# Regrouping the tokens of a feed-forward stage to 512, 320 and 256, with one joint product for the smallest group

## Chip, cores and metric

The kernel runs on one core of one Trainium2 chip. The metric is device time in microseconds (us) of one execution, as the median of several runs. The engines are named as the profile names them: PE is TensorE (matmul), PEld its weight loads, DVE VectorE, ACT ScalarE, POOL GpSimd, SP the engine that issues most DMAs.

## What is computed

One decoder layer over 1088 tokens (1024 of a prompt and 8 samples of 8), with D = 1024 and a hidden width of 2816. The stages are a half-step feed-forward layer, a token mixer (a gated linear recurrence and gated linear attention), cross-attention over 256 memory tokens, a second half-step feed-forward layer, and a final norm:

```
x = x + 0.5 * swiglu_ffn(x, p['ffn1_norm'], p['ffn1_w_gate'], p['ffn1_w_up'], p['ffn1_w_down'])
x = x + mix                       # token mixer
x = x + cross_attend(x, mem_k, mem_v, ...)
x = x + 0.5 * swiglu_ffn(x, p['ffn2_norm'], p['ffn2_w_gate'], p['ffn2_w_up'], p['ffn2_w_down'])
y = rmsnorm(x, p['final_norm'])

def swiglu_ffn(x, g, w_gate, w_up, w_down):
    h = rmsnorm(x, g)
    return (jax.nn.silu(h @ w_gate) * (h @ w_up)) @ w_down
```

Everything is float32. The kernel reaches this precision with split operands: a value v is held as a rounded half `hi` and a rest `lo = v - hi`, and a product is made of three matmuls, w_hi by x_hi, w_hi by x_lo, and w_lo by x_hi.

## The kernel before

**Layout.** x lies in SBUF as `x[128, 8, 1088]`: features on the partitions in 8 blocks k, tokens along the row. A product for one block of 128 output features runs over the 8 blocks k with three matmuls each (`split_mm`, lines L1736, L1737, L1738). The moving operand of each is the activation, so a matmul has as many columns as its group has tokens. The tokens are in three groups n = 0, 1, 2 of 384, 384 and 320 (`NS`), in the whole kernel.

**A feed-forward stage** (`ffn(f)`, f = 0 and 1, on every engine) is 11 iterations `it`; each takes two hidden blocks ft = 0, 1 of 128 features. Three parts follow each other on PE:

- Six gate/up steps s. A step is one hidden block for one group: a gate product u = 0 and an up product u = 1, 8 x 3 matmuls each, into the PSUM banks 4 + 2(s%2) + u. In iteration 0 the order is (ft, n) = (0,0), (1,0), (0,1), (1,1), (0,2), (1,2); in the others (0,0), (0,1), (0,2), (1,0), (1,1), (1,2).
- The work on a finished step. ACT makes the silu of the gate (L849, `sil`), DVE multiplies it with the up product in PSUM (L1296, `hf`), then splits it: a cast to `h_hi` (L1300) and a subtraction to `h_lo` (L1302). Before it takes the banks of step s again, PE waits for the multiplication of two steps before.
- Down products: for n = 0, 1, 2 and each of 8 output blocks m, 6 matmuls into bank m%4; DVE adds half of it to x (L1310, `add`). The product m may start only when the addition of four products before is done, since it takes that bank. The products of group n wait for the `h_lo` of that group.

**Weights.** Each iteration loads six tiles of 128 x 1024 (slots 0 to 3 gate and up, 4 and 5 down). ACT rounds each to `w_hi` (L772, `prep`), POOL subtracts to `w_lo` (L696, `low`). Slots 2 and 3 of the next iteration are loaded when the last gate/up step is done. In stage f = 0, while it = 0 to 9, ACT and POOL also split six tiles of the later stages' weights in each iteration (L783 and L701, `stage_prep` and `stage_low`), three of them right behind slots 2 and 3.

**Norms.** A group's norm is: squares (ACT, L810), sums of eight squared rows (DVE L1144 and L1145, or POOL L730 and L732), sums over partitions (PE, L1763), root (ACT, L823) and reciprocal (DVE, L1137), a spread of the scale to all partitions (PE, L1785), then the scaled rows (DVE, L1215; L1169 in the mixer; L1244 for the final norm) and their split (ACT L838, DVE L1227). In iteration 0 the norms of groups 1 and 2 stand between the steps; in the last iteration the next stage's norm of group 0 stands between the additions of groups 1 and 2, the final norm's rows of group 0 between the additions of group 2.

**What sets the order.** Every engine's program is written out by hand, in order; the engines meet at semaphores. Nothing is rearranged by a scheduler.

## Time and profile before

| what | value |
|---|---|
| median of 3 runs | 2379.21 us (2378.66 to 2383.64) |
| span of the profiled execution | 2379.0 us |
| mean granted TensorE clock | 0.995 |
| PE busy | 2343.7 us (99%), 14996 matmuls |
| DVE busy | 1062.5 us (45%) |
| ACT busy | 494.6 us (21%) |
| POOL busy | 519.1 us (22%) |

The span runs from the first to the last instruction and is 0.2 us below the median of the runs. Stage f = 0 lies from 0 to about 811 us, the mixer and the attention up to about 1567 us, stage f = 1 behind them up to the last additions at about 2364 us. Matmuls are pipelined, so the busy time of one overlaps that of the next: how long one costs is read from the distance between two starts, not from its duration. L12 is line 12 of the kernel.

### The profile page before, as it was taken

What the parts mean: (1) busy time and instruction counts of PE and PEld (TensorE: products, weight loads), DVE (VectorE), ACT (ScalarE), POOL (GpSimd) and SP (SyncE); (2) the same over time, 40 slices, a digit from 0 to 9 for tenths busy, and PEclk for the clock granted to TensorE, in tenths of its full rate; (3) what the DMA queues carried; (4) which work ended last, traced back from release to release, by engine and by line L of the source; (5) the groups of instructions that cost most, each with busy time, mean ns of one, the idle gap of its engine ahead of it and who ended that gap; (6) DMA issues with size and microseconds to landing.
All of it is one profiled execution on the core that took longest, in us unless ns stands there. A gap on an engine that the chain in (4) does not pass through costs nothing. (4 is left out here: it accounts for less than half of the span.)

```text
span 2379.0 us, 36652 instructions
## 1 busy us (share of the span) xinstructions
PE 2343.7 (99%) x14996; PEld 2285.3 (96%) x14996; DVE 1062.5 (45%) x1696; ACT 494.6 (21%) x697; POOL 519.1 (22%) x239
## 2 busy tenths in 40 slices
PE   7999999999999999999999999999999999999998
PEld 7999999999999989899889999799999999999998
DVE  6434334444334574565642423444443344443345
ACT  4222212122211241321410221331111011111101
POOL 2444334344432000000001000022221222221121
PEclk9999999999999999999999999999999999999999
DMA  4554454454452465666678376731101010111112
GB/s 158 213 212 168 159 194 175 151 212 168 159 194 89 156 214 182 212 222 240 231 261 316 145 254 252 276 110 54 53 36 53 35 53 35 53 35 53 35 36 76
DMA packets 89475, 352.50 MB, mean 148 GB/s; under 512 B 8944, under 2 KB 16432, under 8 KB 79152
## 3 DMA queue, kind: packets, MB, share of 16 engines
q1 hardware_dynamic: 89104, 351.12, 40.3%
q8 instruction: 64, 1.05, 0.2%
q10 hardware_dynamic: 288, 0.18, 0.0%
q14 instruction: 19, 0.16, 0.0%
HBM read 280.54 MB, written 70.72 MB: 148 GB/s over the span
## 5 line engine op out<-in xcount | busy, mean ns | idle before, releaser
L1736 PE MATMUL ps<-a_hi,w_sb 128*128 128x384 f32 (+1 forms) x2112 | 691.6, 327 | 6.6 <-DVE a_lo L1227 4.6
L1738 PE MATMUL ps<-a_hi,w_sb 128*128 128x384 f32 (+1 forms) x2112 | 689.9, 327 | 0.0
L1737 PE MATMUL ps<-a_lo,w_sb 128*128 128x384 f32 (+1 forms) x2112 | 689.7, 327 | 0.0
L696 POOL TENSOR_TENSOR w_sb<-w_raw,w_sb 128x1024 fp32r<-128x1024 f32 x132 | 317.7, 2415 | 1066.4 <-ACT w_sb L772 1066.4
L1736 PEld LDWEIGHTS ps<-a_hi,w_sb 128*128 128x128 f32 x2112 | 397.7, 188 | 8.3 <-issue 3.5
L1737 PEld LDWEIGHTS ps<-a_lo,w_sb 128*128 128x128 f32 x2112 | 397.8, 188 | 0.0
L1738 PEld LDWEIGHTS ps<-a_hi,w_sb 128*128 128x128 f32 x2112 | 397.6, 188 | 0.0
L1310 DVE SCALAR_TENSOR_TENSOR x<-ps,x 128x384 f32<-128x384 f32 (+1 forms) x528 | 279.2, 534 | 199.7 <-PE ps L1738 199.7
L1296 DVE TENSOR_TENSOR hf<-sil,ps 128x384 f32<-128x384 f32 x132 | 70.1, 531 | 646.9 <-ACT sil L849 646.9
L1736 PE MATMUL ps<-h_hi,w_sb 128*128 128x384 f32 (+1 forms) x1056 | 344.7, 326 | 0.0
L1738 PE MATMUL ps<-h_hi,w_sb 128*128 128x384 f32 (+1 forms) x1056 | 344.2, 326 | 0.0
L1737 PE MATMUL ps<-h_lo,w_sb 128*128 128x384 f32 (+1 forms) x1056 | 344.1, 326 | 0.0
L849 ACT ACTIVATE sil<-ps 128x384 f32<-128x384 f32 x132 | 62.4, 473 | 1125.8 <-PE ps L1738 1125.7
L1302 DVE TENSOR_TENSOR h_lo<-hf,h_hi 128x384 fp32r<-128x384 f32 x132 | 239.5, 1815 | 4.6
L1736 PEld LDWEIGHTS ps<-h_hi,w_sb 128*128 128x128 f32 x1056 | 198.3, 188 | 0.3 <-DVE x L1310 0.3
L1737 PEld LDWEIGHTS ps<-h_lo,w_sb 128*128 128x128 f32 x1056 | 198.2, 188 | 0.0
L1738 PEld LDWEIGHTS ps<-h_hi,w_sb 128*128 128x128 f32 x1056 | 198.2, 188 | 0.0
L730 POOL TENSOR_TENSOR sq<-sq 128x768 f32<-128x768 f32 (+2 forms) x18 | 31.8, 1769 | 691.9 <-ACT sq L810 691.9
L772 ACT ACTIVATE w_sb<-w_raw 128x1024 fp32r<-128x1024 f32 x132 | 139.1, 1056 | 101.8 <-DMA w_raw<-in_ffn_gate 92.7
L701 POOL TENSOR_TENSOR st_w<-st_raw,st_w 128x1024 fp32r<-128x1024 f32 x60 | 145.2, 2448 | 48.8 <-ACT st_w L783 48.8
L1736 PE MATMUL ps<-mo_hi,w_sb 128*128 128x384 f32 (+1 forms) x384 | 125.7, 327 | 0.7 <-DVE mo_lo L1676 0.7
L1738 PE MATMUL ps<-mo_hi,w_sb 128*128 128x384 f32 (+1 forms) x384 | 125.1, 326 | 0.0
(262 smaller groups left out, 2717.2 us busy)
## 6 DMA issues: line engine op xcount, KB each, us to landing
w_sb<-split SPq DMA_DIRECT2D x148, 1024.0 KB, 5.2
split<-st_w SPq DMA_DIRECT2D x60, 1024.0 KB, 4.1
st_raw<-in_mix_tiles SPq DMA_DIRECT2D x60, 512.0 KB, 5.9
w_raw<-in_ffn_gate SPq DMA_DIRECT2D x44, 512.0 KB, 3.6
w_raw<-in_ffn_up SPq DMA_DIRECT2D x44, 512.0 KB, 4.4
w_raw<-in_ffn_down SPq DMA_DIRECT2D x44, 512.0 KB, 4.3
kc<-in_cache_k SPq DMA_DIRECT2D x5, 1024.0 KB, 8.5
kc<-in_cache_v SPq DMA_DIRECT2D x4, 1024.0 KB, 9.6
```

Source lines behind the costliest of these rows:

```text
L696: nc.gpsimd.tensor_tensor(w_lo_sb[:, slot_, :], raw[:, slot_, :], w_hi_sb[:, slot_, :].bitcast(F32), ALU.subtract)\
L701: nc.gpsimd.tensor_tensor(st_w[:, j % 3, 1, :], st_raw[:, j % 3, 1, :], st_w[:, j % 3, 0, :].bitcast(F32), ALU.subtract)\
L730: nc.gpsimd.tensor_tensor(buf[:, 0:2, 0:p.N], buf[:, 0:2, 0:p.N], buf[:, 2:4, 0:p.N], ALU.add).then_inc(pool_half, 1)
L772: nc.scalar.activation(w_hi_sb[:, slot_, :], raw[:, slot_, :], ACT.Copy).then_inc(w_hi, 1)
L849: nc.scalar.activation(sil[:, s % 2, 0:N], ps[:, 4 + 2 * (s % 2), 0:N], ACT.Silu).then_inc(silu_done, 1)
L1296: nc.vector.tensor_tensor(hf[:, s % 2, 0:N], sil[:, s % 2, 0:N], ps[:, b + 1, 0:N], ALU.mult).then_inc(h_done, 1)
L1302: nc.vector.tensor_tensor(h_lo[ft][:, tokens(n)], hf[:, s % 2, 0:N], h_hi[ft][:, tokens(n)].bitcast(F32), ALU.subtract)\
L1310: nc.vector.scalar_tensor_tensor(out=x[:, m, tokens(n)], in0=ps[:, m % 4, 0:NS[n]], scalar=0.5, in1=x[:, m, tokens(n)], op0=ALU.mult, op1= ...
L1736: nc.tensor.matmul(dst, w_h, x_h, start=start, stop=False)
L1737: nc.tensor.matmul(dst, w_h, x_l, start=False, stop=False)
L1738: return nc.tensor.matmul(dst, w_l, x_h, start=False, stop=stop)
```

## The change

In the two feed-forward stages and the final norm the groups are now 512, 320 and 256 tokens (`FNS`, `ftokens`); mixer and attention keep 384, 384 and 320.

The two halves of group 2's activations lie behind each other in one tile `a_both`. Its gate and up products are made by `joint_mm`: one matmul of w_hi with both halves, 512 columns into one bank (columns 0 to 255 are w_hi by x_hi, 256 to 511 w_hi by x_lo), and one of w_lo with x_hi, 256 columns into the first half. The halves of the bank are added afterwards: ACT copies columns 256 to 511 of both banks to `part`, DVE adds them onto columns 0 to 255, and only then come the silu and the multiplication.

`sil` is one buffer instead of two. The cast and the subtraction of step 5 (`hidden(5, 1, 2)`) stand behind the eight additions of group 0, not ahead of them. What the norms wait for follows the new borders: the norm of group 0 of stage f = 1 waits for the attention output of groups 0 and 1, that of group 1 for part of group 2 and, with its second half, all of it. The squares get buffers that fit.

```diff
+FOFFS = [0, 512, 832]
+FNS = [512, 320, 256]
@@ wait_source
             elif kind == "ffn2":
-                eng.wait_ge(evicted, FIRST["co", n] + 8)
+                eng.wait_ge(evicted, FIRST["co", min(n + 1, 2)] + (4 if n == 1 else 8))
@@ sync: x is loaded by the new groups
-                sp.dma_start(x[:, 4 * h:4 * h + 4, tokens(0)], ...
+                sp.dma_start(x[:, 4 * h:4 * h + 4, ftokens(0)], ...
@@ scalar, norm_squares
                     elif q == 0:
                         wait_source(act, kind, n)
+                    elif (kind, n) == ("ffn2", 1):
+                        act.wait_ge(evicted, FIRST["co", 2] + 8)
@@ scalar, ffn
                 def step(q0, s, first):
                     _, n = ffn_step(first, s)
                     act.wait_ge(gu_done, f * GATE_UP_STEPS + q0 + s + 1)
-                    if f or not first or s >= 2:
-                        act.wait_ge(h_done, f * GATE_UP_STEPS + q0 + s - 1)
-                    N = NS[n]
-                    nc.scalar.activation(sil[:, s % 2, 0:N], ps[:, 4 + 2 * (s % 2), 0:N], ACT.Silu).then_inc(silu_done, 1)
+                    if f or not first or s >= 1:
+                        act.wait_ge(h_done, f * GATE_UP_STEPS + q0 + s)
+                    N = FNS[n]
+                    b = 4 + 2 * (s % 2)
+                    if n == 2:
+                        ft, _ = ffn_step(first, s)
+                        nc.scalar.activation(part[:, :, :], ps[:, b:b + 2, N:2 * N], ACT.Copy).then_inc(part_out, 1)
+                        act.wait_ge(whole_out, f * 2 * ITS + q0 // 6 * 2 + ft + 1)
+                    nc.scalar.activation(sil[:, 0:N], ps[:, b, 0:N], ACT.Silu).then_inc(silu_done, 1)
@@ vector, ffn
+                    def hidden(s, ft, n):
+                        if f or not first:
+                            dve.wait_ge(down_done, X + Q * it - Q + KT * (n + 1))
+                        dve.wait_ge(h_done, G + q0 + s + 1)
+                        nc.vector.tensor_copy(h_hi[ft][:, ftokens(n)], hf[:, s % 2, 0:FNS[n]]).then_inc(hhi_done, 1)
+                        dve.wait_ge(hhi_done, G + q0 + s + 1)
+                        nc.vector.tensor_tensor(h_lo[ft][:, ftokens(n)], hf[:, s % 2, 0:FNS[n]], h_hi[ft][:, ftokens(n)].bitcast(F32), ALU.subtract)\
+                          .then_inc(hid_done, 1)
+
                         b = 4 + 2 * (s % 2)
+                        if n == 2:
+                            dve.wait_ge(part_out, f * 2 * ITS + 2 * it + ft + 1)
+                            nc.vector.tensor_tensor(ps[:, b:b + 2, 0:N], part[:, :, :], ps[:, b:b + 2, 0:N], ALU.add).then_inc(whole_out, 1)
                         dve.wait_ge(silu_done, G + q0 + s + 1)
...
+                        nc.vector.tensor_tensor(hf[:, s % 2, 0:N], sil[:, 0:N], ps[:, b + 1, 0:N], ALU.mult).then_inc(h_done, 1)
+                        if s < 5:
+                            hidden(s, ft, n)
                     for n in range(3):
+                        if n == 1:
+                            hidden(5, 1, 2)
@@ vector, cross-attention output of group 2
-                    if n == 2 and j == 4:
+                    if n == 2 and j == 6:
                         norm_sum("ffn2", 1, 0)
@@ tensor
+            def joint_mm(dst, w_h, w_l, x_both, start, stop):
+
+                N = x_both.shape[2]
+                nc.tensor.matmul(dst[:, 0:2 * N].rearrange("p (a n) -> p a n", a=2), w_h, x_both, start=start, stop=False)
+                return nc.tensor.matmul(dst[:, 0:N], w_l, x_both[:, 0], start=False, stop=stop)
@@ tensor, ffn
-                                ins = split_mm(ps[:, 4 + 2 * (s % 2) + u, 0:NS[n]], w_hi_sb[:, w, c], w_lo_sb[:, w, c],
-                                               a_hi[n][:, k, :], a_lo[n][:, k, :], k == 0, k == KT - 1)
+                                if n == 2:
+                                    ins = joint_mm(ps[:, b, :], w_hi_sb[:, w, c], w_lo_sb[:, w, c], a_both[:, :, k, :], k == 0, k == KT - 1)
+                                else:
+                                    ins = split_mm(ps[:, b, 0:FNS[n]], w_hi_sb[:, w, c], w_lo_sb[:, w, c],
+                                                   a_hi[n][:, k, :], a_lo[n][:, k, :], k == 0, k == KT - 1)
```

**PE, a gate product of group 2 in a middle iteration.** `w_sb` is the weight, a_hi_67 and a_lo_68 are the halves of group 2. Before:

```order
L1736 MATMUL ps<-a_hi_67,w_sb 128x320
L1737 MATMUL ps<-a_lo_68,w_sb 128x320
L1738 MATMUL ps<-a_hi_67,w_sb 128x320
L1736 MATMUL ps<-a_hi_67,w_sb 128x320
L1737 MATMUL ps<-a_lo_68,w_sb 128x320
L1738 MATMUL ps<-a_hi_67,w_sb 128x320
```

And now, for the same two blocks k and one more:

```order
L1783 MATMUL ps<-a_both,w_sb 128x512
L1784 MATMUL ps<-a_both,w_sb 128x256
L1783 MATMUL ps<-a_both,w_sb 128x512
L1784 MATMUL ps<-a_both,w_sb 128x256
L1783 MATMUL ps<-a_both,w_sb 128x512
L1784 MATMUL ps<-a_both,w_sb 128x256
```

Two matmuls stand where three stood; a group of 256 in the old form would also have taken three.

**DVE, from the last gate/up step of iteration 0 through the additions.** (The middle iterations have the same order, with register instructions between.) Before:

```order
L1296 TENSOR_TENSOR hf<-sil,ps 128x320 [waits hid_done,silu_done]
L1300 CAST h_hi_72<-hf 128x320 [waits h_done]
L1302 TENSOR_TENSOR h_lo_73<-hf,h_hi_72 128x320 [waits hhi_done]
L1310 SCALAR_TENSOR_TENSOR x<-ps,x 128x384 [waits down_done] x16
L1310 SCALAR_TENSOR_TENSOR x<-ps,x 128x320 [waits down_done] x8
```

Now:

```order
L1334 TENSOR_TENSOR ps<-part,ps 128x2x256 [waits part_out]
L1338 TENSOR_TENSOR hf<-sil,ps 128x256 [waits hid_done,silu_done]
L1350 SCALAR_TENSOR_TENSOR x<-ps,x 128x512 [waits down_done] x8
L1311 CAST h_hi_73<-hf 128x256 [waits h_done]
L1313 TENSOR_TENSOR h_lo_74<-hf,h_hi_73 128x256 [waits hhi_done]
L1350 SCALAR_TENSOR_TENSOR x<-ps,x 128x320 [waits down_done] x8
L1350 SCALAR_TENSOR_TENSOR x<-ps,x 128x256 [waits down_done] x8
```

An addition in PSUM has come in ahead of the multiplication, and cast and subtraction have moved past the eight additions of group 0.

**ACT, the last gate/up step of a middle iteration.** Before:

```order
L849 ACTIVATE sil<-ps 128x384
L772 ACTIVATE w_sb<-w_raw 128x1024
L845 REGISTER_ALU
L849 ACTIVATE sil<-ps 128x320
L772 ACTIVATE w_sb<-w_raw 128x1024 x2
```

Now:

```order
L877 ACTIVATE sil<-ps 128x320
L793 ACTIVATE w_sb<-w_raw 128x1024
L868 REGISTER_ALU
L875 ACTIVATE part<-ps 128x512
L876 REGISTER_ALU
L877 ACTIVATE sil<-ps 128x256
L793 ACTIVATE w_sb<-w_raw 128x1024 x2
```

The copy to `part` is new, ahead of the silu and of the weights of slots 2 and 3.

## Rows read from the trace of the kernel before

**Rows 1.** Page, costliest groups: operation, count | busy us, mean ns | idle.

```profile
L1736 PE MATMUL ps<-a_hi,w_sb 128*128 128x384 f32 (+1 forms) x2112 | 691.6, 327 | 6.6 <-DVE a_lo L1227 4.6
```

**Rows 2.** Windows: stretch; PE, PEld, DVE, ACT, POOL busy; clock; DMA.

```profile
97.00:736.00 639.00, 639.00 (x3884) 639.00 (x3883) 266.21 (x377) 130.10 (x162) 263.19 (x110) 1.00 0.48 182
1575.00:1590.00 15.00, 12.53 (x61) 12.12 (x60) 8.79 (x14) 7.20 (x10) 5.00 (x2) 0.77 0.01 2
```

**Rows 3.** Timeline, PE: start, length; pairs at 256, 384, 512 columns.

```profile
1221.05 0.28 PE L1736 MATMUL ps<-xm_hi,w_sb 128*128 128x256 f32 x1
...
1224.65 0.28 PE L1736 MATMUL ps<-xm_hi,w_sb 128*128 128x256 f32 x1
...
384.39 0.33 PE L1736 MATMUL ps<-a_hi,w_sb 128*128 128x384 f32 x1
...
387.51 0.33 PE L1736 MATMUL ps<-a_hi,w_sb 128*128 128x384 f32 x1
...
1235.67 0.39 PE L1900 MATMUL ps<-w_sb,xm_hi 128*128 128x512 f32 x1
...
1240.43 0.39 PE L1900 MATMUL ps<-w_sb,xm_hi 128*128 128x512 f32 x1
```

**Rows 4.** Timeline, stage f = 0, down products of it = 5; last row of it = 7.

```profile
428.65 0.34 PE L1736 MATMUL ps<-h_hi,w_sb 128*128 128x384 f32 x1
...
433.12 0.56 DVE L1310 SCALAR_TENSOR_TENSOR x<-ps,x 128x384 f32<-128x384 f32 x1 [0.48 <-PE ps L1738]
...
433.65 4.79 POOL L696 TENSOR_TENSOR w_sb<-w_raw,w_sb 128x1024 fp32r<-128x1024 f32 x2 [7.92 <-ACT w_sb L772]
438.39 7.11 POOL L701 TENSOR_TENSOR st_w<-st_raw,st_w 128x1024 fp32r<-128x1024 f32 x3
...
580.24 7.12 POOL L701 TENSOR_TENSOR st_w<-st_raw,st_w 128x1024 fp32r<-128x1024 f32 x3
```

**Rows 5.** Timeline, DVE beside POOL in iteration 0; last row without POOL, it = 5.

```profile
61.73 7.27 POOL L701 TENSOR_TENSOR st_w<-st_raw,st_w 128x1024 fp32r<-128x1024 f32 x3 [7.60 <-ACT st_w L783]
...
65.98 0.75 DVE L1300 CAST h_hi<-hf 128x384 fp32r<-128x384 f32 x1
...
66.76 2.65 DVE L1302 TENSOR_TENSOR h_lo<-hf,h_hi 128x384 fp32r<-128x384 f32 x1
...
430.27 0.49 DVE L1302 TENSOR_TENSOR h_lo<-hf,h_hi 128x320 fp32r<-128x320 f32 x1
```

**Rows 6.** Timeline, start of the program, up to PE's first gate matmul.

```profile
7.96 1.48 ACT L810 ACTIVATE sq_b<-x 128x1536 f32<-128x1536 f32 x1 [0.76 <-DMA x<-in_x]
...
11.08 1.44 PE L1763 MATMUL ps<-cst,sq_b 128*128 128x1 f32 x6 [0.74 <-DVE sq_b L1145]
...
14.83 2.19 DVE L1215 SCALAR_TENSOR_TENSOR frow<-x,vec,ps 128x384 f32<-128x384 f32 x4 [1.74 <-PE ps L1785]
...
18.07 0.66 PE L1736 MATMUL ps<-a_hi,w_sb 128*128 128x384 f32 x1 [3.28 <-DVE a_lo L1227]
```

**Rows 7.** Timeline, start of stage f = 1, POOL and PE.

```profile
1575.13 5.00 POOL L696 TENSOR_TENSOR w_sb<-w_raw,w_sb 128x1024 fp32r<-128x1024 f32 x2 [8.14 <-ACT w_sb L772]
...
1577.98 0.83 PE L1763 MATMUL ps<-cst,sq_b 128*128 128x1 f32 x6 [1.10 <-DVE sq_b L1145]
1580.18 0.69 PE L1736 MATMUL ps<-a_hi,w_sb 128*128 128x384 f32 x1 [1.37 <-POOL w_sb L696]
```

**Rows 8.** Timeline, iteration 0 of f = 1: DVE, then PE in step 4.

```profile
1604.28 2.66 DVE L1302 TENSOR_TENSOR h_lo<-hf,h_hi 128x384 fp32r<-128x384 f32 x1
...
1613.11 0.41 PE L1736 MATMUL ps<-a_hi,w_sb 128*128 128x320 f32 x1 [0.64 <-DVE a_lo L1227]
```

**Rows 9.** Timeline, PE, the mixer's first matmul.

```profile
811.20 0.41 PE L1736 MATMUL ps<-xn_hi,w_sb 128*128 128x384 f32 x1 [0.73 <-issue]
```

**Rows 10.** Timeline, DVE, last iteration of f = 1 and the last rows.

```profile
2347.21 0.96 DVE L1144 TENSOR_TENSOR sq<-sq 128x768 f32<-128x768 f32 x1 [0.52 <-ACT sq L810]
...
2369.19 5.83 DVE L1244 SCALAR_TENSOR_TENSOR yb<-x,vec,ps 128x384 f32<-128x384 f32 x12
```

More of the change, by code:

```diff
@@ L35 @@
 NMAX = 384
+FOFFS = [0, 512, 832]
+FNS = [512, 320, 256]
+FMAX = 512
 NPROMPT = [384, 384, 256]
@@ L476, in tokens, with ftokens, group @@
             return slice(OFFS[n], OFFS[n] + NS[n])
+        def ftokens(n):
+            return slice(FOFFS[n], FOFFS[n] + FNS[n])
+        def group(kind, n):
+            return ftokens(n) if kind in ("ffn1", "ffn2", "fin") else tokens(n)
         def norm_source(kind, n, q):
@@ L484, in norm_source @@
                 return osb[:, :, 0:N]
-            return (memx if kind == "mem" else x)[:, 4 * q:4 * q + 4, slice(0, N) if kind == "mem" else tokens(n)]
+            return (memx if kind == "mem" else x)[:, 4 * q:4 * q + 4, slice(0, N) if kind == "mem" else group(kind, n)]
         GATE_UP_STEPS = 6 * ITS
```

75 lines of the change are left out of this document (39 added, 36 removed).

## The prediction, made before the result was known

> **What bounds the kernel now.** I read the windows first. From 97 to 736 us, nine whole iterations of stage f = 0, PE is busy 639.00 of 639.00 us at full granted clock, DVE 266, POOL 263 [rows 2]. So in the loops PE alone sets the time. A change there is worth what it takes off PE's stream, as long as nobody starts to make PE wait. Outside the loops PE waits at a few places, and these depend on how wide group 0 is [rows 6 to 10].
>
> The price of a matmul is the distance of two starts. At 256 columns 30 matmuls take 3.60 us, 120.0 ns each; at 384 columns 18 take 3.12 us, 173.3 ns; at 512 columns 21 take 4.76 us, 226.7 ns [rows 3]. The clock granted there is full, 2.4 GHz. All three are (columns + 32) / 2.4 GHz: each matmul has a fixed part of 13.3 ns, whatever its width. An iteration has 432 matmuls and 156,672 columns, which gives 71.04 us.
>
> **A. The joint product: -9.4 us.** The columns per block k stay 3 x 1088; the matmuls go from 9 to 8. The x2112 of [rows 1] is 44 hidden blocks x 2 products x 8 k x 3 groups, so 704 are saved: 704 x 13.3 ns = 9.4 us, 0.43 us in each of 22 iterations. Down products keep their count. No row shows a moving operand in two pieces of 256 columns. Dearest, the two pieces cost like two matmuls, and A is 0; nothing in the rows lets it fall below -9.4. I take -9.4, since output and count of columns are those of an ordinary 512-column matmul [rows 3].
>
> The Trainium skill, page "TensorE: Matmul & The Clock Gate", section "Back-to-back issue gap", speaks against this gain: it gives N/2.4 + 2.5 ns at full clock. By it A would be 704 x 2.5 ns = 1.8 us. The trace disagrees, with 13.3 ns at three widths.
>
> ACT's copy and DVE's addition lengthen the way from a finished step to its h by about 1.3 us (0.6 + 0.7, taken from 512-wide neighbours of the 0.56 us of a 384-wide operation [rows 4]). They cost nothing: PE needs those banks again only after the next step, 7 us or more in the middle iterations. ACT has `prep` and `stage_prep` queued behind, and slots 2 and 3 are in the air until after that.
>
> **B. Last h behind the additions: +8.6 us.** The critical place is the middle iterations of f = 0. Call U the start of the down products, 428.65 in [rows 4]. A product m of group 0 takes 6 x 226.7 ns = 1.36 us, so group 0 ends at U + 10.88. DVE starts an addition 0.31 us behind the product's end (433.12 is U + 4.47, the fourth product ended at U + 4.16 [rows 4]). The last one, 0.70 us at 512 tokens less 0.06 of overlap, lets the cast begin at U + 11.83, which is 440.48.
>
> What POOL does then is [rows 4]: two `low` to 438.4, then three `stage_low` of 2.4 us, starting at 438.39, 440.75 and 443.1. And [rows 5] shows how DVE fares beside such a row of POOL operations. The cast (0.75 us in place of 0.36) got through between the second and the third. The subtraction had to wait for the whole third, and ended 0.42 us behind it (66.76 + 2.65 against 69.00); alone it takes 0.49 at 320 columns. Additions that read PSUM are not held up (0.56 us at 433.12, in the middle of POOL's work [rows 4]).
>
> So: the cast gets through at 440.8, the subtraction ends 0.28 us (0.42 less 128/0.96 ns for the smaller width) behind the second `stage_low`, which the cast pushes to 443.27: 443.55. The addition 0 of group 1 starts 0.08 us before that, takes 0.49 and ends at 443.96, PE could go on at 444.01. PE wants it for product m = 4 of group 1, at U + 10.88 + 4 x 6 x 146.7 ns = U + 14.40 = 443.05 (320 columns cost 352/2.4 ns by [rows 3]). The stall is 0.96 us, in nine iterations (it = 1 to 9): 8.6 us. Before, the same step ran at U + 1.3, ahead of POOL's work. In f = 1 there is no `stage_low`, and POOL is done at U + 10: free. In iteration 0 the weights come later than U + 11.8: free.
>
> Bounds: where POOL is as early as at 580.24 (U = 570.85, so its first `stage_low` ends at U + 11.79 [rows 4]), the cast misses the gap, the subtraction ends behind the third operation, and the stall is 0.96 + 2.05 = 3.0 us. Otherwise the ends in the nine iterations lie at 11.97 to 12.28. From below, the subtraction gets in right behind the cast: no stall. So 0 to 27 us, and I take 0.96 each.
>
> **C. The start: +4.0 us.** The first two loads of x grow by a third. The second landed at about 7.96, with the first 1.57 MB in all [rows 6]; at 2.10 MB it is +1.5. Squares, 1.48 us for 1536 elements, +0.45; the two sums +0.4; PE's column sums and spread, 8 small matmuls for 6, +0.9 over both; four scaled rows (2.19 us [rows 6]) and the first split, +0.8. Together +4.1 on the first gate matmul, 18.07 before. The pairs then arrive slower (+0.3), and a wait of 0.36 us for slots 2 and 3 goes, since the first step is 2.6 us longer. +4.0; between +3 and +5.
>
> **D. Start of f = 1: -3.7 us.** Before, PE waited twice, 1.10 and 1.37 us idle and some more to refill, for the sums of group 1 and for the weights of slots 2 and 3 [rows 7], 3.1 us in all, and then ran at 1.2 GHz: the window from 1575 has a mean clock of 0.77 [rows 2], worth about 2.1 us. The product that covers the waits grows from 4.16 to 5.44 us twice. The sums are then in time; POOL's 5 us pair starts 0.9 us later and ends at 1581.1, against 1579.6 when PE gets there. 1.5 us remain, and no other wait lies beside it: at 1613.11 a single wait of 0.64 [rows 8] did not lower the clock. 1.5 against 5.2 is -3.7; with the clock still falling -1.6.
>
> **E. Step 4 of iteration 0, twice: +1.0 us.** PE stood 0.8 us there (0.64 idle [rows 8]) for the split of group 2. The step before is 1.3 us shorter, the split itself gets 1.1 us shorter, but four blocks k of step 4 last 1.4 us and not 1.8, and every pair is late: +1.1. If the subtraction ahead (2.66 us beside POOL [rows 8]) comes ahead of POOL's operation, 2.2 us are gained, and this is -0.8. The margin shrinks to about 0.03 us in f = 1, and turns in f = 0, where a shorter step 4 then waits 0.7 us for its banks. +1.1 and -0.1; range -1 to +3.
>
> **F. Into the mixer: +1.1 us.** In the last iteration of each stage, group 0 ends 2.56 us later and groups 1 and 2 are 1.28 us shorter each. DVE's chain from the end of group 0 to the next stage does not shorten as much. For f = 0 the chain to the mixer's first matmul (811.20 [rows 9], 18.55 us behind the end of group 0) shortens to 17.1. +2.56 - 1.45 = +1.1; 0 to +2.
>
> **G. The tail: +3.1 us.** In f = 1 the squares of group 0 wait for the last h too. They end 3.5 us after the end of group 0 (2.1 before), the sum of 0.96 us [rows 10] becomes 1.24, and PE waits 2.1 us at m = 4. Behind it narrower rows of the final norm (12 rows in 5.83 us [rows 10] become 5.2) give most of it back: the distance from the end of group 0 to the last row stays near 30 us (+0.5). With the 2.56: +3.1; +2 to +4. A fourth spread column in the attention adds 0.3.
>
> **Sum.** -9.4 + 8.6 + 4.0 - 3.7 + 1.0 + 1.1 + 3.1 + 0.3 = +5.0. The profiled 2379.0 us become 2384.0, and the median, 0.2 above it, 2384.2.
>
> **Rivals.**
> - *The cover holds*: B is 0. It decides whether the subtraction ends before U + 13.9; for it speaks only that iteration 0 showed one case of the pattern [rows 5]. 2384.2 - 8.6 = 2375.6. Chance 0.20.
> - *The cast misses the gap* in several iterations, 2.05 us each: four give 2392, all nine 2402.6. It needs `stage_low` 0.4 us earlier than usual; one of nine was. 0.15.
> - *The joint matmul saves nothing* (two pieces cost like two): 2384.2 + 9.4 = 2393.6. 0.08.
> - *Fixed part of 2.5 ns*: A shrinks to 1.8 us, 2391.8. The three widths are against it. 0.02. This is the Trainium skill's rule named above.
> - *Faster*: B is 0 and start and tail cost half (3.5 less): 2372.1. 0.05.
>
> **How the numbers follow.** The forecast has 0.50, by itself 2380.5 to 2387.5. A measurement can tell about 0.2% from no change, 4.8 us: faster is below 2374.4, slower above 2384.0. The forecast's half splits 0.28 slower, 0.22 same; the first rival 0.14 same, 0.06 faster; the next three, 0.25, are slower; the last 0.05 faster. Faster 0.11, same 0.36, slower 0.53. The range takes in the first rival and most of the second and third: 2374.5 to 2394.
>
> **What would show it.** A: in a middle iteration of f = 1, 70.6 us instead of 71.1 between two first gate matmuls, and 346.7 ns for a pair of joint matmuls. B: one wait of PE of nearly 1 us in each of nine iterations of f = 0, ended by an addition (L1350), with a subtraction (L1313) of some 2.4 us before it; iterations of 71.6 us. C: first gate matmul at 22.2. D: no clock of 1.2 GHz near 1585. F, G: waits of PE at m = 4 of the last iterations. I am wrong if f = 0 runs as fast as f = 1, or if the pair costs 360 ns.

## The result, and the profile of the changed kernel

The changed kernel takes 2393.8 us (median of 4 runs, 2393.1 to 2395.4) against 2380.0 us before (4 runs, 2378.7 to 2383.6): ratio 1.0050, 95% interval 1.0036 to 1.0064. It is slower by 0.5%. The direction was right, and the time lies inside the range (2374.5 to 2394) by 0.2 us; the size was not right: +5.0 us forecast, +13.8 measured. The profiled span is 2392.7 us against 2379.0, so +13.7 is what the traces have to explain. One execution of the kernel with three repairs (below) took 3878 us at a mean granted clock of 0.557 and is left out of that kernel's numbers.

The page, costliest groups, now has the plain product of groups 0 and 1 in L1776 and the joint one in L1783 and L1784 (the rows answer to [rows 1]):

```profile
L1776 PE MATMUL ps<-a_hi,w_sb 128*128 128x320 f32 (+1 forms) x1408 | 494.5, 351 | 6.3 <-DVE a_lo L1255 4.0
...
L1783 PE MATMUL ps<-a_both,w_sb 128*128 128x512 f32 x704 | 250.9, 399 | 2.3 <-DVE a_both L1255 1.7
...
L1784 PE MATMUL ps<-a_both,w_sb 128*128 128x256 f32 x704 | 197.7, 281 | 0.0
```

704 matmuls are gone, as the change says. The windows (columns as in [rows 2]) are f = 0 beyond its first iteration, the start of f = 1 and a stretch of the tail:

```profile
103.00:750.00 647.00, 639.97 (x3595) 572.38 (x3595) 259.03 (x395) 140.81 (x180) 270.85 (x110) 1.00 0.47 179
...
1580.00:1595.00 15.00, 13.42 (x67) 11.14 (x65) 3.29 (x5) 5.11 (x6) 5.52 (x3) 1.00 0.32 112
2360.00:2375.00 15.00, 12.96 (x91) 12.80 (x91) 10.85 (x21) 5.72 (x5) 3.85 (x3) 0.89 0.00 1
```

In f = 0 PE is no longer busy all the time: 7.0 of 647 us are missing. The view of PE's waits from 100 to 760 us has one line, the sum, the number and the longest of them:

```profile
PE ps L1776 <- DVE x L1350: 7.0, 9, 1.1
```

So that an account can be made, here are PE's first matmuls of iterations 1 and 10 of both stages, and the attention's last one (timeline):

```profile
102.59 0.40 PE L1776 MATMUL ps<-a_hi,w_sb 128*128 128x512 f32 x1
...
750.55 0.40 PE L1776 MATMUL ps<-a_hi,w_sb 128*128 128x512 f32 x1
...
1580.67 0.31 PE L1778 MATMUL ps<-mo_hi,w_sb 128*128 128x320 f32 x1
...
1659.62 0.40 PE L1776 MATMUL ps<-a_hi,w_sb 128*128 128x512 f32 x1
...
2298.20 0.40 PE L1776 MATMUL ps<-a_hi,w_sb 128*128 128x512 f32 x1
```

The same places before: 96.85, 736.75, 1566.69, 1649.25, 2289.15 us. With the terms of the prediction put into the same stretches (A is -0.43 an iteration; E lies in the first and in the fourth stretch):

| stretch | before | after | measured | forecast |
|---|---|---|---|---|
| start to iteration 1 | 96.85 | 102.59 | +5.7 | +3.5 |
| f = 0, iterations 1 to 9 | 639.90 | 647.96 | +8.1 | +4.7 |
| to the attention's last matmul | 829.94 | 830.12 | +0.2 | +1.0 |
| to iteration 1 of f = 1 | 82.56 | 78.95 | -3.6 | -3.0 |
| f = 1, iterations 1 to 9 | 639.90 | 638.58 | -1.3 | -3.9 |
| iteration 10 and tail | 89.9 | 94.5 | +4.6 | +2.7 |
| sum | 2379.0 | 2392.7 | +13.7 | +5.0 |

The short stretches are not the same in every profile. The kernel with a measuring row (below) is the changed kernel up to its end: its first gate matmul comes at 23.80 us (24.27 here) and its iteration 1 at 102.18. In the third stretch lie the mixer and the attention, which the change leaves nearly alone, and a fall of the clock. The window 1190 to 1230 us, before and then after:

```profile
1190.00:1230.00 40.00, 39.23 (x385) 37.13 (x384) 15.10 (x39) 8.54 (x14) 0.00 (x0) 0.91 0.61 225
```

```profile
1190.00:1230.00 40.00, 39.38 (x450) 37.05 (x450) 12.52 (x41) 6.50 (x14) 1.31 (x2) 0.96 0.52 188
```

Over the kernels with the new groups the third stretch lies between 829.5 and 831.7 us. The mixer's first matmul shows how much of it the change made (timeline, after; before [rows 9]):

```profile
826.41 0.41 PE L1776 MATMUL ps<-xn_hi,w_sb 128*128 128x384 f32 x1 [0.93 <-issue]
```

That is 75.86 us behind the start of iteration 10, against 74.45 before.

**The waits in f = 0.** DVE, POOL and PE (timeline) in iteration 2, whose down products start at 221.85 us (the rows answer to [rows 4, 5]):

```profile
233.00 0.69 DVE L1350 SCALAR_TENSOR_TENSOR x<-ps,x 128x512 f32<-128x512 f32 x1 [0.58 <-PE ps L1778]
233.60 0.56 DVE L1311 CAST h_hi<-hf 128x256 fp32r<-128x256 f32 x1
234.20 2.52 DVE L1313 TENSOR_TENSOR h_lo<-hf,h_hi 128x256 fp32r<-128x256 f32 x1
236.64 2.29 DVE L1350 SCALAR_TENSOR_TENSOR x<-ps,x 128x320 f32<-128x320 f32 x5
...
226.87 4.78 POOL L717 TENSOR_TENSOR w_sb<-w_raw,w_sb 128x1024 fp32r<-128x1024 f32 x2 [6.30 <-ACT w_sb L793]
231.59 7.37 POOL L722 TENSOR_TENSOR st_w<-st_raw,st_w 128x1024 fp32r<-128x1024 f32 x3
...
237.18 0.41 PE L1776 MATMUL ps<-h_hi,w_sb 128*128 128x320 f32 x1 [0.70 <-DVE x L1350]
```

The row of POOL merges three `stage_low` of about 2.46 us. The cast gets through near the end of the first (231.59 + 2.46 = 234.05), the subtraction is held for the whole second one and ends at 236.72, the addition behind it at 237.1, and PE stands. All nine iterations show this order. With U, as in the prediction, for the start of the down products: the cast starts at U + 11.75, and the first `stage_low` ends between U + 12.01 and U + 12.56. In f = 1, where POOL has no `stage_low`, the same two instructions are short:

```profile
1931.45 0.28 DVE L1311 CAST h_hi<-hf 128x256 fp32r<-128x256 f32 x1
1931.77 0.42 DVE L1313 TENSOR_TENSOR h_lo<-hf,h_hi 128x256 fp32r<-128x256 f32 x1
```

**The joint product.** PE, first and sixteenth 512-column matmul of two products that follow each other (timeline):

```profile
1890.42 0.39 PE L1783 MATMUL ps<-a_both,w_sb 128*128 128x512 f32 x1
...
1895.72 0.40 PE L1783 MATMUL ps<-a_both,w_sb 128*128 128x512 f32 x1
```

Fifteen pairs take 5.30 us, 353 ns each, where 226.7 + 120.0 = 346.7 were forecast [rows 3]. In iteration 0 of f = 1 the same instructions, in the same order, run faster (PE, two 512-column matmuls, sixteen pairs apart):

```profile
1627.59 0.39 PE L1783 MATMUL ps<-a_both,w_sb 128*128 128x512 f32 x1
...
1633.13 0.39 PE L1783 MATMUL ps<-a_both,w_sb 128*128 128x512 f32 x1
```

Sixteen pairs in 5.54 us are 346 to 347 ns each. So the joint pair has two steady prices in one and the same kernel; all the middle iterations have the dear one.

**The start** (answers to [rows 6]). POOL, DVE, PE:

```profile
12.62 5.18 POOL L717 TENSOR_TENSOR w_sb<-w_raw,w_sb 128x1024 fp32r<-128x1024 f32 x2 [12.17 <-ACT w_sb L793]
...
12.89 2.71 DVE L1173 TENSOR_TENSOR sq_e<-sq_e 128x512 f32<-128x512 f32 x1
...
24.27 0.77 PE L1776 MATMUL ps<-a_hi,w_sb 128*128 128x512 f32 x1 [4.04 <-DVE a_lo L1255]
```

**Step 4 in f = 0, start of f = 1, step 4, and tail** (PE; answers to [rows 7, 8, 10]), then DVE's last rows of the final norm:

```profile
68.04 0.50 PE L1783 MATMUL ps<-a_both,w_sb 128*128 128x512 f32 x1 [0.45 <-DVE a_both L1255]
...
73.22 0.50 PE L1783 MATMUL ps<-a_both,w_sb 128*128 128x512 f32 x1 [0.65 <-DVE hf L1338]
...
1595.58 0.50 PE L1776 MATMUL ps<-a_hi,w_sb 128*128 128x512 f32 x1 [1.29 <-POOL w_sb L717]
...
1625.99 0.51 PE L1783 MATMUL ps<-a_both,w_sb 128*128 128x512 f32 x1 [0.54 <-DVE a_both L1255]
...
2362.07 1.02 PE L1809 MATMUL ps<-cst,sq 128*128 128x1 f32 x8 [2.04 <-DVE sq L1173]
...
2384.03 5.04 DVE L1272 SCALAR_TENSOR_TENSOR yb<-x,vec,ps 128x320 f32<-128x320 f32 x12
```

One wait is left at the start of f = 1, and the clock stays at 1.00 from 1580 (0.77 before [rows 2]). At the tail PE waits 2.04 us, and from 2360 the clock is 0.89.

### The profile page after: what moved, and what is told of

The parts are those of the page before. It is cut to its first block and busy times, and to the rows that moved or that the text cites. A ratio compares the mean times of both kernels' runs of the same rounds, so it can differ in the third digit from the quotient of the medians.

```text
span 2392.7 us, 35406 instructions
## 1 busy us (share of the span) xinstructions
PE 2342.2 (98%) x14292; PEld 2121.0 (89%) x14292; DVE 1048.5 (44%) x1740; ACT 519.8 (22%) x741; POOL 534.1 (22%) x239
## 5 line engine op out<-in xcount | busy, mean ns | idle before, releaser
L1776 PE MATMUL ps<-a_hi,w_sb 128*128 128x320 f32 (+1 forms) x1408 | 494.5, 351 | 6.3 <-DVE a_lo L1255 4.0
L1778 PE MATMUL ps<-a_hi,w_sb 128*128 128x320 f32 (+1 forms) x1408 | 492.5, 350 | 0.0
L1777 PE MATMUL ps<-a_lo,w_sb 128*128 128x320 f32 (+1 forms) x1408 | 492.5, 350 | 0.0
L1776 PE MATMUL ps<-h_hi,w_sb 128*128 128x512 f32 (+2 forms) x1056 | 347.9, 329 | 7.7 <-DVE x L1350 7.7
L1350 DVE SCALAR_TENSOR_TENSOR x<-ps,x 128x512 f32<-128x512 f32 (+2 forms) x528 | 278.9, 534 | 173.8 <-PE ps L1778 170.4
L1778 PE MATMUL ps<-h_hi,w_sb 128*128 128x512 f32 (+2 forms) x1056 | 346.3, 328 | 0.0
L1777 PE MATMUL ps<-h_lo,w_sb 128*128 128x512 f32 (+2 forms) x1056 | 345.9, 328 | 0.0
L1776 PEld LDWEIGHTS ps<-a_hi,w_sb 128*128 128x128 f32 x1408 | 264.9, 188 | 36.2 <-issue 4.3
L1778 PEld LDWEIGHTS ps<-a_hi,w_sb 128*128 128x128 f32 x1408 | 264.7, 188 | 28.6
L1777 PEld LDWEIGHTS ps<-a_lo,w_sb 128*128 128x128 f32 x1408 | 265.1, 188 | 27.7
L1783 PE MATMUL ps<-a_both,w_sb 128*128 128x512 f32 x704 | 250.9, 399 | 2.3 <-DVE a_both L1255 1.7
L1776 PEld LDWEIGHTS ps<-h_hi,w_sb 128*128 128x128 f32 x1056 | 200.0, 189 | 25.1 <-DVE x L1350 10.2
L1784 PE MATMUL ps<-a_both,w_sb 128*128 128x256 f32 x704 | 197.7, 281 | 0.0
L1313 DVE TENSOR_TENSOR h_lo<-hf,h_hi 128x512 fp32r<-128x512 f32 (+1 forms) x132 | 193.4, 1465 | 4.6
L1783 PEld LDWEIGHTS ps<-a_both,w_sb 128*128 128x128 f32 x704 | 132.2, 188 | 34.6 <-DVE a_both L1255 2.4
```

Source lines behind the costliest of these rows:

```text
L1313: nc.vector.tensor_tensor(h_lo[ft][:, ftokens(n)], hf[:, s % 2, 0:FNS[n]], h_hi[ft][:, ftokens(n)].bitcast(F32), ALU.subtract)\
L1350: nc.vector.scalar_tensor_tensor(out=x[:, m, ftokens(n)], in0=ps[:, m % 4, 0:FNS[n]], scalar=0.5, in1=x[:, m, ftokens(n)], op0=ALU.mult, o ...
L1776: nc.tensor.matmul(dst, w_h, x_h, start=start, stop=False)
L1777: nc.tensor.matmul(dst, w_h, x_l, start=False, stop=False)
L1778: return nc.tensor.matmul(dst, w_l, x_h, start=False, stop=stop)
L1783: nc.tensor.matmul(dst[:, 0:2 * N].rearrange("p (a n) -> p a n", a=2), w_h, x_both, start=start, stop=False)
```

## Experiments

All edits are to the changed kernel unless it says otherwise. Where an edit is given in words or with "...", it stands for a longer one. Each time is a median of several runs (the measuring row ran once), but each trace is of one execution.

### The last h back ahead of the additions

```
-                        if s < 5:
-                            hidden(s, ft, n)
+                        hidden(s, ft, n)
                     for n in range(3):
-                        if n == 1:
-                            hidden(5, 1, 2)
```

> The changed kernel with one part undone: the last h of an iteration is split into halves ahead of the additions again, in both stages. Theory (the late split is what makes PE wait): the nine waits of 0.7 to 1.3 us at the fifth product of group 1 in f = 0 are gone, an iteration of f = 0 lasts 71.0 us as one of f = 1 does (72.0 in the changed kernel), and the last iterations lose their waits at the same place: 9.4 us less in the loops and some 2 us at the tail, 2382 to 2385 us in all. Rival (the widths of the groups, 512 columns in group 0, are what makes DVE late): the waits move to another product of group 0 or 1 but stay near 1 us, 2392 to 2395 us.

2386.2 us, ratio to before 1.0025 (1.0015 to 1.0036). The view of PE's waits in f = 0 is empty. PE, iterations 1 and 10:

```profile
102.66 0.40 PE L1772 MATMUL ps<-a_hi,w_sb 128*128 128x512 f32 x1
...
741.24 0.40 PE L1772 MATMUL ps<-a_hi,w_sb 128*128 128x512 f32 x1
```

638.58 us for nine iterations, 70.95 each: 9.4 us less than 647.96. The rival falls. The late split costs 9.4 us in the loops of f = 0. The whole kernel gains less, 7.7 us by the medians, and the 2 us expected at the tail did not come: by the profiles the stretch between the loops got 1.6 us longer and the tail 0.8. The 1.6 us go with the clock in the attention (0.91 from 1190 to 1230 us, 0.96 in the changed kernel). At the tail PE is idle for 1.29 us where it was 2.04, but the clock from 2350 to 2360 falls to 0.76.

### POOL's operations moved away from the late split

```
                     if f == 0:
+                        pool.wait_ge(hid_done, 6 * it + 6)
                         for j in range(3, 6):
                             stage_low(it, j)
```

> The changed kernel; POOL waits in f = 0 for the last h's subtraction before it starts its second three stage_low operations, so that no long POOL operation runs beside DVE's cast and subtraction. Theory (the subtraction waits for a whole POOL operation): cast 0.28 and subtraction 0.42 us as in f = 1, no wait of PE at the fifth product of group 1, iterations of f = 0 at 70.95 us, 9.4 us less than the changed kernel, 2384.4 us. Rival (the order of DVE's work alone makes the addition late): the waits stay near 1 us, or are half as long, and the kernel stays above 2389.

2387.7 us, ratio 1.0028 (1.0018 to 1.0039). DVE and POOL at the same place:

```profile
232.12 0.28 DVE L1312 CAST h_hi<-hf 128x256 fp32r<-128x256 f32 x1
232.44 0.42 DVE L1314 TENSOR_TENSOR h_lo<-hf,h_hi 128x256 fp32r<-128x256 f32 x1
...
233.03 7.14 POOL L722 TENSOR_TENSOR st_w<-st_raw,st_w 128x1024 fp32r<-128x1024 f32 x3 [2.97 <-DVE h_lo L1314]
```

The split stays late, every iteration of f = 0 lasts 70.95 us, and PE has no wait. So it is not the order of DVE's work but POOL's operation beside the subtraction that makes the addition late. The 9.4 us expected off the loops came; by the profiles 3.0 us were lost again behind them, 1.4 between the loops (again with a clock of 0.91 from 1190 to 1230) and 1.6 at the tail (96.1 us from iteration 10 in place of 94.5), where the clock from 2350 to 2360 was 0.76.

The Trainium skill, page "SBUF — State Buffer", section "Who interferes with whom", says which pairs get in each other's way: a DVE instruction with two inputs in SBUF contends with a GpSimd instruction that reads SBUF, since its second input comes through a read interface that both share, and that sharing is an exclusive lock; a DVE instruction with at most one input in SBUF, outside the modes that take both ports, doesn't contend. By that rule the subtraction is held and an addition with one input in PSUM is not; the traces agree (subtraction 2.52 against 0.42 us; addition of 512 tokens 0.69 us beside POOL at 233.00 and 0.69 us at 1930.84, where POOL is idle).

### The late split alone, on the kernel before

The same edit as in the change, with groups of 384, 384, 320 and three matmuls per block.

> The kernel before with the late split alone (groups 384, 384, 320, three products). Group 0 of the down products ends at U + 8.3, the last addition at U + 9.2, PE wants the first addition of group 1 at U + 12.5. Theory (what the late split costs depends on where in POOL's row it falls): cast in the gap at U + 9.6, subtraction behind the first stage_low, ended near U + 12.3, addition 0.56 us, so PE waits 0.3 to 0.5 us in nine iterations, 71.4 to 71.6 us each in f = 0, and 71.10 in f = 1; with up to 1 us at the tail 2383 to 2386 us. Rival 1 (a late split costs 0.96 us wherever it falls): 72.1, 2389 us. Rival 2 (only 512 columns make it late): 71.10 and 2380.

2387.9 us, ratio 1.0035 (1.0022 to 1.0047). DVE, then POOL, in iteration 2 (down products from 216.58 us):

```profile
225.60 1.12 DVE L1283 CAST h_hi<-hf 128x320 fp32r<-128x320 f32 x1
226.75 2.57 DVE L1285 TENSOR_TENSOR h_lo<-hf,h_hi 128x320 fp32r<-128x320 f32 x1
...
226.46 7.46 POOL L701 TENSOR_TENSOR st_w<-st_raw,st_w 128x1024 fp32r<-128x1024 f32 x3
```

Nine waits, the first matmul behind each 0.58 to 0.76 us late, iterations of 71.79 to 71.99 us, 7.1 us in all. The mechanism is that of the theory (cast at the end of POOL's first pair, subtraction behind the first `stage_low`); the size was short by about half, since the two instructions end at 229.32, U + 12.7, and not at U + 12.3. Rival 2 falls; of the late split's price 512 columns are only a part. Rival 1 is not far off by its size (0.79 us an iteration measured, 0.96 by the rival); what speaks against it is the kernel with groups of 384, 448, 256 below, where the subtraction is held just as long (2.5 us) and PE doesn't wait.

### Gate and up of group 2 as three matmuls

> The changed kernel with gate and up of group 2 as three 256-column matmuls per block k again; ACT's copy and DVE's addition are gone. Theory (a matmul has a fixed part of 13.3 ns, but the joint one loses half of it again): three take 360.0 ns against 353.0 for the joint pair, so a middle iteration of f = 1 goes from 70.95 to 71.17 us and the kernel gets 4.9 us slower, near 2398.7. Rival 1 (the whole 13.3 ns is saved, and the 512-column groups lose it elsewhere): 71.38 us an iteration, 2403. Rival 2 (the joint matmul saves nothing): 70.95, and 2393.8 unchanged.

2399.9 us, ratio 1.0087 (1.0070 to 1.0104). In f = 1 an iteration takes 71.10 us, exactly as before the change, and not the 71.17, 71.38 or 70.95 expected. So the joint product is worth 0.147 us an iteration (71.10 less 70.95, before rounding), 3.2 us in 22, a third of the 9.4 of step A. The trace shows the parts of an iteration: the two hidden blocks' joint products take 11.30 us where the three-matmul ones take 11.52, 0.22 less, and each of the two rows of 48 matmuls of 512 columns behind a joint product takes 10.94 us in place of 10.91. The whole time came near the theory's 2398.7, but partly by luck: the loops account for 3.2 of the 6.1 us between the two medians.

### The joint matmul reads one piece

```
-        a_both, o = at("a_both", [P, 2, KT, FNS[2]], o, F32R)
+        a_both, o = at("a_both", [P, KT, 2 * FNS[2]], o, F32R)
```

> The changed kernel with both halves of a of group 2 side by side for each block k, so that the joint matmul reads one piece of 512 columns in place of two pieces of 256 that lie 8 KB apart. Theory T (reading two pieces costs 6 to 9 ns a matmul): the 512-column matmul falls from 236 to 226.7 ns, the pair from 353.0 to 346.7 or less, a middle iteration of f = 1 from 70.95 to 70.75, the kernel to 2389.4 us. Rival S (going from 256 to 512 columns and back costs it, whatever the layout): 353.0 ns, 70.95 us and 2393.8 stay.

Pairs of 353.0 ns and iterations of 70.95 us, as with two pieces: theory T falls. The time was 2399.0 us, ratio 1.0085 (1.0068 to 1.0101), 5 us above the changed kernel although its loops of f = 1 are the same and those of f = 0 0.8 us shorter. In the profile the difference lies where PE waits and the clock falls: 1.8 us at the start of f = 1 and 3.0 at the tail. The window 2360 to 2375 of this kernel:

```profile
2360.00:2375.00 15.00, 12.97 (x64) 12.71 (x63) 7.48 (x13) 5.55 (x6) 0.45 (x1) 0.66 0.00 1
```

0.66 against 0.89, and 0.90 against 1.00 from 1595 to 1610. Why all four runs of this kernel were above 2398 us was not found out.

### The wide matmuls first

```
-  for k: joint_mm(512 columns of w_hi; 256 columns of w_lo)
+  for k: 512 columns of w_hi
+  for k: 256 columns of w_lo
```

> The changed kernel with the order of the joint product changed: first its eight 512-column matmuls, then its eight 256-column ones, in place of one and one in turn. Rival S (each change from narrow to wide costs about 7 ns): the seven changes inside a product go, the wide ones take 226.7 ns and the narrow ones 120.0 (346.7 for both), an iteration of f = 1 lasts 70.75 us in place of 70.95, the kernel 2389.4. Theory T (two pieces cost it): the wide ones stay at 236 ns or more, and nothing changes, 2393.8.

PE, first 512-column matmul of two products in a row:

```profile
1891.75 0.39 PE L1784 MATMUL ps<-a_both,w_sb 128*128 128x512 f32 x1
...
1894.54 0.40 PE L1784 MATMUL ps<-a_both,w_sb 128*128 128x512 f32 x1
```

2.79 us a product, 348.7 ns a pair (346.7 expected: the first five wide ones of a product take 228 to 236 ns each), and 70.75 us an iteration in f = 1: the 0.2 us came as rival S said. So in the middle iterations the order sets the price, and the layout doesn't. But the two kinds in turn don't always cost it, as the pairs of iteration 0 show (346 to 347 ns). The time is 2394.1 us (ratio 1.0057, 1.0041 to 1.0074), no gain: here too the clock fell at the edges (0.89 from 1595, 0.77 from 2360).

### Groups of 384, 448, 256

```
-FNS = [512, 320, 256]
+FNS = [384, 448, 256]
```

> The changed kernel with groups of 384, 448 and 256 tokens in place of 512, 320 and 256; joint product and late split stay. Theory (start, tail and the nine waits hang on the width of group 0): the first gate matmul is back near 18 us and iteration 1 starts near 97 us (102.6 in the changed kernel). Group 0 of the down products ends at U + 8.3, PE wants the first addition of group 1 4.8 us later (3.5 with 320 columns), and the subtraction is due right behind the first stage_low at U + 12.3: no wait of PE, iterations of f = 0 at 70.95 us. With 3 us less at the tail and in the mixer it is 2375 to 2379 us, as the kernel before or faster. Rival (any late split collides with POOL's row of operations): f = 0 stays at 71.8 to 72.5 us an iteration, 2384 to 2390 us.

2393.4 us, ratio 1.0061 (1.0044 to 1.0078). Iteration 1 starts at 98.16 us, and there is no wait in the middle iterations of f = 0, both near what the theory said. But the time lies outside both forecasts, 14 us above the theory's: an iteration lasts 71.57 us (71.5 to 71.6 in f = 0), 0.62 more than in the changed kernel for the same columns and the same number of matmuls. The trace shows where: 48 matmuls of 448 columns take 9.91 us, 206.5 ns each, not (448 + 32) / 2.4 = 200.0. An iteration has three such rows, which cost 0.94 us more. About a third of it comes back: the 32 pairs take 346.7 ns each here (15 in 5.20 us), 0.20 us less, and rows of 512 columns, which lay 0.03 to 0.06 us above the line in the changed kernel, are gone.

```profile
1886.15 0.40 PE L1783 MATMUL ps<-a_both,w_sb 128*128 128x512 f32 x1
...
1891.35 0.39 PE L1783 MATMUL ps<-a_both,w_sb 128*128 128x512 f32 x1
```

### A row of widths

A measuring row on PE behind the kernel's end, 36 matmuls of a width, then pairs.

> The changed kernel with a measuring row of matmuls appended on PE behind everything else (its outputs don't use it, so its time is not compared): 36 matmuls each of 256, 288, 320, 352, 384, 416, 448, 480 and 512 columns, then pairs of 512 and 256 columns behind 36 of 320, of 448 and of 512, then 24 of 512 behind 36 of 256, of 320 and of 384. Theory L (a fixed part of 13.3 ns at every width): 120.0, 133.3, 146.7, 160.0, 173.3, 186.7, 200.0, 213.3 and 226.7 ns; the 206.7 ns at 448 columns with groups of 384, 448 and 256 came from something else in that kernel. Theory W (the fixed part depends on the width): 206.7 ns at 448 here as well, and other odd widths off the line too. For the pairs: theory S (what came before the row decides how long 512 columns take): 353 ns behind 320 columns and 347 behind 448 columns; rival: the same in all three places. For 512 columns behind narrower ones: about 60 ns more in all behind 320 columns, spread over the first eight or so.

PE at 448 columns, the fifth and the thirty-fifth matmul:

```profile
2440.31 0.37 PE L2347 MATMUL ps<-h_lo,w_sb 128*128 128x448 f32 x1
...
2446.51 0.37 PE L2347 MATMUL ps<-h_lo,w_sb 128*128 128x448 f32 x1
```

| columns | 256 | 288 | 320 | 352 | 384 | 416 | 448 | 480 | 512 |
|---|---|---|---|---|---|---|---|---|---|
| ns | 120.0 | 131.6 | 146.7 | 160.0 | 173.3 | 188.3 | 206.7 | 216.7 | 226.7 |
| (columns + 32) / 2.4 | 120.0 | 133.3 | 146.7 | 160.0 | 173.3 | 186.7 | 200.0 | 213.3 | 226.7 |

Theory W holds: 448 columns cost 6.7 ns more, 480 3.3 and 416 1.6. The three widths of [rows 3] happened to lie on the line. In a second row of 448, further on, they took 202.7 ns in a steady pattern, so the width alone doesn't fix the price. The pairs settled at 353.3 ns in all three places: theory S falls here. Why they take 346.7 in the kernel with 384, 448, 256 and in iteration 0 of the changed one is open. 512 columns behind narrower ones took 25 to 46 ns more in all before they settled at 226.7, 25 of them behind 320 columns, where 60 were expected.

### POOL behind the first sums

```
                 if f == 0:
+                    pool.wait_ge(summed, 2)
                 for k in range(4):
                     low(k, before + k + 1)
```

> The changed kernel; POOL starts its first operations (low halves of slots 0 and 1) only behind DVE's two sums of squares of group 0, which at 12.9 us took 2.71 us in place of 0.7 beside POOL. Theory (that subtraction beside the sum is what the start lost beyond the wider group): the second sum takes 0.7 us, the first gate matmul comes at 22.2 us in place of 24.3, and POOL's two operations end near 19 us, ahead of it; the kernel 2391.8 us. Rival (another wait, for the data of x or of the weights, stands right behind): the first gate matmul stays within 0.5 us of 24.3 and the time at 2393.8.

DVE, POOL, PE:

```profile
12.37 0.69 DVE L1175 TENSOR_TENSOR sq_e<-sq_e 128x512 f32<-128x512 f32 x1
...
13.14 4.65 POOL L717 TENSOR_TENSOR w_sb<-w_raw,w_sb 128x1024 fp32r<-128x1024 f32 x2 [12.69 <-DVE sq_e L1175]
...
21.73 0.77 PE L1778 MATMUL ps<-a_hi,w_sb 128*128 128x512 f32 x1 [4.04 <-DVE a_lo L1257]
```

The first gate matmul comes 2.5 us sooner (2.1 against the 23.80 of the kernel with a measuring row) and iteration 1 starts at 100.13: the theory holds. The time, 2393.6 us (2391.1 to 2397.8; ratio 1.0060, 1.0042 to 1.0078), doesn't show it: the window 2360 to 2375 had a clock of 0.77 in this kernel's profile, and the tail was 1.6 us longer.

### Three repairs together (e11), and the tail (e12)

The split ahead of the additions, the wide matmuls first, POOL behind the sums:

> The changed kernel with three repairs at once: last h split ahead of the additions, the eight 512-column matmuls of a joint product ahead of its eight 256-column ones, POOL's first operations behind the sums of the first norm. Theory (the three are independent, each as seen alone): iteration 1 starts near 99.8 us, all iterations of both stages last 70.75 us in place of 72.0 and 70.95, 2.4 + 4.2 + 9.4 us less than the changed kernel in all, 2377 to 2380 us, within 0.2% of the kernel before. Rival (the shorter loops turn into waits at the edges, at the start of f = 1 and the tail, where the clock falls): 2381 to 2385 us.

2383.4 us (median of nine runs), ratio 1.0008 (0.9998 to 1.0019). Both stages run at 70.75 us an iteration and iteration 1 starts at 100.60. The profiled span is 2379.8 us, but the runs lie between 2377.4 (mean clock 0.997) and 2387.1 (0.992), in the order of their clocks. The loops gained what the theory said; the median lies in the rival's range. What the loops gain, the edges can lose.

Then PE's column sums in the last iteration later (e12):

```
-  last iteration: column sums ahead of m = 4 and m = 6 of group 1, spread ahead of m = 1 of group 2
+  last iteration: column sums ahead of m = 6 of group 1 and m = 0 of group 2, spread ahead of m = 2
```

> The combined kernel (last h split ahead of the additions, 512-column matmuls of a joint product first, POOL behind the first sums), and in the last iteration of each stage PE's column sums of group 0 moved: from ahead of products 4 and 6 of group 1 to ahead of product 6 of group 1 and product 0 of group 2, the spread from product 1 to product 2. Theory (a wait of PE of 1.5 us at 2346 lengthens the tail by itself and lets the clock fall to 1.2 GHz behind it, where the window from 2350 showed 0.66 of full clock): the wait is gone, the clock there stays at 1.0, and start of iteration 10 of f = 1 to the end takes 90 to 92 us in place of 94.9, 2378 to 2381 us. Rival (the final norm's chain on ACT and DVE sets the end, PE's wait lay beside it): the stretch stays within 1 us of 94.9, 2382 to 2384 us.

2379.5 us, ratio 0.9996 (0.9986 to 1.0005). The window 2350 to 2360, first of the kernel with three repairs, then with the sums moved too:

```profile
2350.00:2360.00 10.00, 10.00 (x57) 10.00 (x57) 4.57 (x11) 2.70 (x3) 1.85 (x2) 0.66 0.01 2
```

```profile
2350.00:2360.00 10.00, 9.79 (x77) 9.58 (x78) 7.37 (x16) 3.43 (x4) 3.60 (x3) 1.00 0.01 2
```

The clock stays full there, and iteration 10 with the tail takes 92.0 us in place of 94.9: the theory holds, and PE's wait at the tail was on the path. The next kernel's profile has 92.0 too, while the eight kernels with groups of 512, 320, 256 and the sums in their old place lie between 93.1 and 97.5. By the medians alone (2379.5 against 2383.4, with runs of the latter 10 us apart) it would not be settled. In the last iteration of f = 0 the same move changed nothing: the mixer's first matmul comes 75.6 us behind the start of iteration 10 in both.

Last, iteration 0 of each stage with the two kinds in turn again (e13):

> As the kernel e12, but iteration 0 of each stage keeps the joint product's matmuls of 512 and 256 columns in turn; only the later iterations have the wide ones first. Theory (the wide ones in a row ask for the pairs of a sooner, so that PE waits longer at 64 us and at 1609 to 1613 us, 0.95 and 2.5 us): these waits fall to those of the changed kernel, 0.6 and 1.7 us, each stage starts iteration 1 about 0.3 us sooner, 0.6 us in all, less than the runs scatter. Rival (the pairs' arrival sets the end of step 4 either way): no change of those stretches.

2378.5 us, ratio 0.9994 (0.9985 to 1.0003). PE's idle time before the pairs of group 2 fell, from 0.78 to 0.45 us in f = 0 and from 1.69 to 1.24 in f = 1. In f = 0 a wait of 0.60 us for the banks of step 5 followed instead, and iteration 1 came no sooner (79.2 us behind the first gate matmul both times). In f = 1 iteration 1 came 0.3 us sooner, as forecast, but that is luck: the clock fell at another place (0.89 from 1575 to 1590 here, 0.91 from 1610 to 1630 in e12), so that one short stretch got 1.6 us longer and the four joint products behind it took 1.9 us less, of which idle time is only 0.45. With all repairs the kernel is level with the one before; nothing tried is measurably faster than it.

## Why the forecast was right in direction and short in size

That the measured 2393.8 us lie inside the range is luck: its upper end was drawn for two rivals that did not occur (the cast misses the gap, the joint matmul saves nothing), and the miss came from A, C, E and G. The time alone would also fit the rival "the joint matmul saves nothing" (2393.6 us); the kernel with three products per block refutes it, since there an iteration is 0.147 us longer.

**A failed**, and it is most of the miss. Forecast -9.4 us, measured -3.2 (71.10 to 70.95 us, 22 times). The count of matmuls fell as said; the step that took the joint matmul for an ordinary 512-column one, at the price read in a row of its own kind, did not hold. A pair in turn takes 353 ns in the middle iterations and not 346.7, 0.20 us an iteration, and the 512-column rows behind it lose another 0.07; that leaves about 0.15 of the 0.43. With the wide ones first 0.35 of the 0.43 us are there. Why the pairs settle at 353 ns is open: the same pairs in turn run at 346.7 in iteration 0 and in the kernel with groups of 384, 448, 256. The range's dear end for A (two pieces cost like two matmuls) would have been 0; the layout, which was suspected there, costs nothing. The small fixed part of the rival (2.5 ns) gives about -1.8 us, nearer to the -3.2 than the forecast; but the wide-first kernel's -0.35 an iteration, 7.6 us in 22, speaks against that rival as the reason. The formula (columns + 32) / 2.4, too, holds for the three widths that it was read from and not for all.

**B held.** Forecast 0.96 us in nine iterations; measured 7.0 us idle, and 9.4 us more in the loops than with the early split, 1.04 each. Order, place and releaser were as described, and POOL's operation is the cause: with it moved away the late split costs nothing in the loops. Neither the rival in which the cover holds nor the one in which the cast misses the gap occurred in any of the nine; in the closest case the gap came 0.26 us behind the earliest possible start of the cast. One reading of B is wrong without harm: the addition at 433.12 us [rows 4] doesn't lie in the middle of POOL's work, which begins at 433.65. That additions aren't held is shown by others (0.69 us at 233.00, beside POOL).

**C was short by 1.3 us, and E in f = 0 by 0.9**, which makes the 2.2 of the first stretch. In C the wider group was sized about right: with POOL behind the sums the first gate matmul comes at 21.73 us, forecast 22.2. What was missed is the collision that B had taught: the sums of group 0 came later and met POOL's first operation (12.62 us); before, that began together with the second sum and didn't hold it (0.56 us at 10.46). E in f = 0 was to be -0.1: -0.8 if the subtraction gets in ahead of POOL, and +0.7 for the banks. It did get in (0.49 us at 61.31), but the scaled rows then waited for PE's spread, and PE still stood 0.45 us for the split, and then 0.65 for the banks, the part that was forecast. Together it is +0.85.

**D, and E in f = 1, held** (-3.6 us together, forecast -3.0; about -4.0 for D and +0.85 for E, forecast -3.7 and +1.1): one wait left, no clock of 1.2 GHz at the start of f = 1 in this profile. In the kernel with one piece, which differs there only in the layout of group 2's activations, the clock did fall (0.90 from 1595 to 1610), and the stretch was 1.8 us longer. **F** came out near its forecast by luck: the third stretch was +0.2, forecast +1.0, but up to the mixer's first matmul it is +1.4 (75.86 against 74.45), forecast +0.7 with A's share, and -1.2 behind it, where the program is nearly the same and the clock was 0.96 in place of 0.91 from 1190 to 1230 us. No term of the forecast stood for that -1.2.

**G was short by 1.9 us.** The wait of 2.1 us at product 4 was right. The step that failed is that narrower rows of the final norm behind it give most of it back: they can't, since the additions of group 1, which that norm waits for, were themselves late behind PE's wait, and the clock fell behind it. Counted from the start of the last addition of group 0, the last of them ends after 13.1 us, against 10.2 before, and the last row of the final norm after 32.5, against 29.9: +2.6 us, where +0.5 was forecast. Moving the sums gave 2.9 us (the kernel e12 against the one with three repairs).

In sum 6.2 (A) + 2.2 (C, and E in f = 0) + 1.9 (G) + 0.8 (B) - 0.8 (F) - 0.6 (D, and E in f = 1) is 9.7; the stretches differ by 8.7 in all. The rest, 1 us, is that A's share of the short stretches is counted in both.

## What to carry to other kernels

Before an operation with two SBUF inputs is moved on DVE, lay its new place beside POOL's row: it is the collision there that sets its length, here 0.42 or 2.52 us. Take the price of a matmul from rows at its own width and in its own order, not from a line through other widths, and let it be a range where such rows disagree. And beside a loop that runs at PE's limit, look at the waits at its edges: here one cost about twice its length, with the clock that fell behind it (2.9 us for an idle time of 1.29). Before a gain at an edge is believed, look at the clock of the same window in other profiles of the same program.
